# An encoder layer with a mixture of experts: one weight load and three row loads are issued at other places of the DMA queue

## The chip, the cores and the metric

One Trainium2 chip; the kernel runs on one of its cores. The time is what the device takes for one execution, in microseconds (us); of several runs the median is given. The core has a tensor engine (PE in the rows, PEld for its weight loads), a vector engine (DVE), a scalar engine (ACT), GpSimd (POOL) and SyncE (SP). In this kernel SP does no arithmetic: it issues DMAs, in the order of its own program, each after the waits that stand ahead of it. POOL issues the DMAs that gather and scatter rows by an index. "Slot" below is one of three places in the on-chip memory that hold the weights of one expert.

## The reference

One layer over two groups of tokens, 512 and 256, each token 1024 wide, float32. What matters here is its last part: a second RMS norm, a router that picks one of 4 groups and two of the 8 experts in it, the 32 SwiGLU experts, a gated residual, and the last RMS norm.

```
h = rms_norm(x, norm2_g) * (1 + sc2) + sh2
gsel = argmax(softmax(h @ rg_w + rg_b))            # one group of 4
top_p, top_i = top_k(softmax(le of that group), 2)  # two experts of its 8
eid = gsel * 8 + top_i                              # 768 tokens, 2 picks each
for each expert e:
    xb = h[tokens of e]
    y = (silu(xb @ w1[e]) * (xb @ w3[e])) @ w2[e]   # w1, w3: 1024x512, w2: 512x1024
    out[token] += weight * y
x = x + g2 * out
return rms_norm(x, final_g)
```

Ahead of it stand the first norm, the input projection, neighbourhood attention on one half of the width, a bidirectional RWKV-7 recurrence on the other, and the output projection.

## The kernel before, in words

The program is written by hand, engine by engine: each engine has one list of instructions per phase, and semaphores alone set the order between engines. Phases 4 to 7 follow each other in one block without a barrier, so an engine walks from one to the next as soon as its own list lets it.

Phase 5 (`sp_phase5`, `dve_phase5`, `pe_phase5`) ends the output projection, makes the second norm, writes the normed rows to the DRAM scratch `h2_dram`, and turns the router's scores into index lists by a long chain of small DVE operations (L2103 to L2182). When `idx_ready` comes (L2159), POOL may gather; when the last weight of a pick is made (L2182), `list_ready` comes, and SP writes the overflow lists to DRAM (L2000 to L2002).

Phase 6 goes over the 32 experts. Each has room for 64 rows. For expert e POOL gathers its 64 rows from `h2_dram` (L2363); PE transposes them (L2459), ACT copies them out of PSUM (L2403); PE multiplies with w1 and then w3 (both L2472), ACT and DVE make the gated product, PE transposes it (L2481) and multiplies with w2 (L2490); DVE copies the result (L2442), and POOL scatters it to DRAM (L2352). The first two gathers wait for nothing but the index; gather e waits until the rows of expert e-2 are transposed.

Each expert has three weights of 2 MB. There are three slots (`NSLOT = 3`), so nine weights can be loaded before any of them is used. Phase 5 issues these nine on SP between its other transfers: `weights(n, slot)` at L1965, n being 0 for w1, 1 for w3, 2 for w2. Of slot 2 the weights 0 and 1 are issued before SP waits for `list_ready`, and weight 2 behind the lists (L2003 in the code, shown at L1965). From then on (`ahead`, L2326) SP loads a weight of expert e+3 as soon as PE has used the same weight of expert e: `sp.wait_ge(sem(name), CREDIT + c.n + 1)`. All these transfers stand in SP's one queue.

Three rows of the last stage, each spread over all 128 partitions (512 KB of writes), are issued at L2342 (`g2_row`, two of them) and L2343 (`f_row`, the final norm's gain), after the loop, once w2 of expert 29 has been used.

Phase 7 reads the scattered results back (L2525, six loads of 1 MB), joins them on PE and DVE, norms, and writes the output (L2528).

Memory is one `arena`, cut by a counter `top[0]`. Slot 2 lies from `ARENA - 2 * WEXP` on. The routing temporaries (`both_e`, `rank16`, `level` and others) are taken one after another from `at_gate` on, and before the change some of them lie in slot 2's region of w2; hence its load stands behind `list_ready`, the end of their use.

Of the kernel before, what the change touches and what calls it, by code (L numbers as in the profile page):

```python
# [21 lines left out]
f16 = mybir.dt.float16  # L22
# [6 lines left out]
P = 128  # L29
D = 1024  # L30
# [3 lines left out]
NT = NT_S + NT_P  # L34
TOK = NT * P
# [9 lines left out]
NE, EPG, NG = 32, 8, 4  # L45
HID = 512
KH = HID // P
BLK = 64
MAX_OVER = 2 * TOK // BLK
NBLK = NE + MAX_OVER  # L50
# [102 lines left out]
def build(nc, A, O, upto=4):  # L153
    ctx = ExitStack()
    with ctx:
# [4 lines left out]
        def sem(name):  # L160
            if name not in sems:
                sems[name] = nc.alloc_semaphore(name=name)
            return sems[name]
# [5 lines left out]
        ARENA = 53200  # L169
        arena = ctx.enter_context(nc.sbuf_tensor("arena", [P, ARENA], f32))  # L170
        top = [0]

        def take(n):
            at = top[0]
            top[0] += n
            assert top[0] <= ARENA, top[0]
            return arena[:, at:at + n]
# [11 lines left out]
        mod_dram = dram("mod_scratch", [2, 6 * D])  # L189
# [13 lines left out]
        at_gate = top[0]  # L203
# [879 lines left out]
        at_prep = top[0]  # L1083
# [785 lines left out]
        g2_row = take(2 * D).rearrange("p (g d) -> p g d", g=2)  # L1869
# [6 lines left out]
        WEXP = 2 * KD * HID + KH * D  # L1876
# [33 lines left out]
        top6 = top[0]  # L1910
# [19 lines left out]
        rank_row, block_row, token_row = part(BLK), part(NBLK), part(2 * NT)  # L1930
        thresholds = part(NE)[0:NE, 0:TOK // BLK - 1]
        half_place = part(1)
        counting = take(P + 1).bitcast(f16)
        before16, ones16 = counting[:, 0:P], counting[:, P:2 * P]
        tri16 = take(NE).bitcast(f16)[0:NE]
        at_both = top[0]
        shifted = arena[:, at_both:at_both + 2 * KD * 36].rearrange("p (g k e) -> p g k e", g=2, k=KD)
        ones32 = hT[:, 4, W:W + P]
        assert at_both + 2 * KD * 36 <= at_gate + NT_S * W, (at_both - at_gate)
        gm, gsum, m1, m2, pk = (take(NT) for _ in range(5))  # L1940
        og, tg = (take(NT * NG).rearrange("p (t g) -> p t g", g=NG) for _ in range(2))
        s8, t8, o1, o2 = (take(NT * 8).rearrange("p (t e) -> p t e", e=8) for _ in range(4))
        N2 = 2 * NT
        both_e = take(N2 * NE).rearrange("p (k t e) -> p k t e", k=2, t=NT)
        tmp_e = arena[:, top6:top6 + N2 * NE].rearrange("p (n e) -> p n e", e=NE)
        wrap = take(NBLK)
        lsel = take(NT * NE).rearrange("p (t e) -> p t e", e=NE)
        hits16 = take(NT * NE // 2).bitcast(f16).rearrange("p (t e) -> p t e", e=NE)
        rank12, first12, excl12, pos12, low12, base12 = (take(N2) for _ in range(6))
        level = take(N2 * (TOK // BLK - 1)).rearrange("p (n m) -> p n m", n=N2)  # L1950
        rank16 = take(N2 * BLK // 2).bitcast(f16).rearrange("p (n s) -> p n s", n=N2)
        block16 = take(N2 * NBLK // 2).bitcast(f16).rearrange("p (n b) -> p n b", n=N2)
        cnt_col, over_col = take(1), take(1)
        over_lvl = take(TOK // BLK)[0:NE, 0:TOK // BLK - 1]
        over16 = take(P // 2).bitcast(f16)[0:NE]
        sums = take(2 * NE)
        o32 = take(NE)
        assert top[0] <= at_prep, top[0]

        WEIGHTS = (("h1_mm", w1_f, w1_v), ("h3_mm", w3_f, w3_v), ("y_mm6", w2_f, w2_v))  # L1960

        def sp_phase5(sp):
            def weights(n, slot_no):
                name, slot, view = WEIGHTS[n]
                sp.dma_start(slot[slot_no], view[slot_no]).then_inc(sem(f"{name}_w{slot_no}"), 16)  # L1965

            def h2_rows(t):
                sp.wait_ge(sem("h2_ready"), t + 1)
                sp.dma_start(h2_dram[t * P:(t + 1) * P, :], h2[t % 2]).then_inc(sem(f"h2_out{t % 2}"), 16)

            sp.wait_ge(sem("rec_tr"), NT_S)
            for dst, src in ((route, A["c_route"]), (counting[:, 0:2 * P], A["c_counting"]), (tri16, A["c_tri16"])):
                sp.dma_start(dst, src).then_inc(sem("consts5_in"), 16)
            sp.wait_ge(sem("y_mm"), STEPS)
            x_rows(sp, 2)
            sp.wait_ge(sem("ss_ready"), 2)
            x_rows(sp, 3)
            h2_rows(0)
            for n in range(3):
                weights(n, 0)  # L1980
            for t in range(NT_S, NT):
                sp.wait_ge(sem(f"rec_tok{t}"), 1)
            for t in range(NT_S, NT):
                x_rows(sp, t)
            sp.wait_ge(sem("router_mm"), 1)
            weights(2, 1)
            for t in range(1, NT - 1):
                h2_rows(t)

            sp.wait_ge(sem("o5_mm"), 2 * NT)  # L1990
            weights(0, 1)
            h2_rows(NT - 1)
            weights(1, 1)
            weights(0, 2)
            sp.wait_ge(sem("router_mm"), NT)
            for q in range(2):
                sp.wait_ge(sem(f"h2_out{q}"), 48)
            weights(1, 2)
            sp.wait_ge(sem("list_ready"), 1)
            sp.dma_start(over_dram, lst_i[0:MAX_OVER, :]).then_inc(sem("list_out"), 16)  # L2000
            sp.dma_start(slot_dram.rearrange("(b s) o -> b (s o)", s=BLK), over_idx[NE:NBLK]).then_inc(sem("list_out"), 16)
            sp.dma_start(put_dram.rearrange("(b s) o -> b (s o)", s=2 * BLK), over_put[NE:NBLK]).then_inc(sem("list_out"), 16)  # L2002
            weights(2, 2)  # L2003

        def pool_phase5(pool):
            pool.wait_ge(sem("h2_out0"), 48)
# [257 lines left out]
        CREDIT = 3  # L2264
# [54 lines left out]
        def sp_phase6(sp):  # L2319
            def ahead(c):  # L2320

                static = isinstance(c.n, int)
                if not static or c.n + NSLOT < NE:
                    for name, slot, view in WEIGHTS:
                        sp.wait_ge(sem(name), CREDIT + c.n + 1)
                        sp.dma_start(slot[c.w], one(view, c.e + NSLOT)).then_inc(sem(f"{name}_w{c.w}"), 16)  # L2326

            turns(sp, ahead, ahead=NSLOT)

            def over(c):  # L2330
                sp.wait_ge(sem("over_done"), c.n + 1)
                sp.dma_start(idx_o[0:BLK, :], slot_dram[bass.ds(c.first_slot, BLK), :]).then_inc(c.sem("idx_in0"), 16)
                sp.dma_start(put_o, put_dram[bass.ds(c.first_slot * 2, 2 * BLK), :]).then_inc(c.sem("idx_in0"), 16)
                for name, slot, view in WEIGHTS:
                    sp.dma_start(slot[0], one(view, c.e)).then_inc(c.sem(f"{name}_w0"), 16)


            sp.wait_ge(sem("list_out"), 48)
            count = overflow_count(sp)
            sp.wait_ge(sem("y_mm6"), CREDIT + NE - 2)  # L2340
            for g in range(2):
                sp.dma_start(g2_row[:, g, :], mod_dram[g, 5 * D:6 * D].partition_broadcast(P)).then_inc(sem("g2_in"), 16)  # L2342
            sp.dma_start(f_row, A["final_row"].partition_broadcast(P)).then_inc(sem("final_in"), 16)  # L2343
            sp.wait_ge(sem("y_mm6"), CREDIT + NE)
            overflow(sp, over, count, with_expert=True)

# [159 lines left out]
        top[0] = ARENA - WEXP  # L2506
        yo = [take(D) for _ in range(NT)]
        top[0] = ARENA - 2 * WEXP
        f_row = take(D)
        sq7 = take(D)  # L2510
        stat7 = take(NT * 4).rearrange("p (t m) -> p t m", t=NT)

# [171 lines left out]
```

## Time and profile before

| what | us |
|---|---|
| median of 3 runs | 1383.43 |
| lowest, highest | 1381.2, 1383.94 |
| span of the profiled execution, first to last instruction | 1375.9 |
| around the span, to the median | 7.5 |
| phase 5's end: last gather before the experts issued at | 825.70 |
| experts: first matmul with w1, last matmul group with w2 | 830.59, 1329.71 |
| mean granted clock of the tensor engine | 0.948 |

The profiled execution's own device time is not among the recorded ones; 7.5 us is the median of the runs less the span. Times in the rows count from the span's start. From 840 to 1320 us, a third of the whole, the DMA engines are busy all the time at some 400 GB/s. Before that there are a few microseconds in which they carry next to nothing.

### The profile page before, as it was taken

Reading aid. Unit: us, or ns where it says so; the run is one execution under the profiler, and the core shown is the slowest. Engines: PE = TensorE matmul, PEld = TensorE weight load, DVE = VectorE, ACT = ScalarE, POOL = GpSimd, SP = SyncE. Lnnn points to the kernel's source line nnn. Section 1 sums busy time; section 2 is a strip of 40 time slices with the busy share of each in tenths; the row PEclk is TensorE's granted clock in tenths of the full one; section 3 lists DMA queues with packets and bytes.
Section 4 is the critical chain, followed back from the end, with each engine's and each line's share of the span. In section 5 each row is a group of like instructions: output and inputs, shape, how many; then the busy total and the mean of one; then the engine's idle time right before and its main releaser. Section 6 shows DMA issues by size and latency. Waiting matters only on the chain.

```text
span 1375.9 us, 29721 instructions
## 1 busy us (share of the span) xinstructions
PE 1178.5 (86%) x13063; PEld 727.2 (53%) x13063; DVE 421.8 (31%) x742; ACT 348.6 (25%) x749; POOL 280.7 (20%) x254
## 2 busy tenths in 40 slices
PE   5899999999997898988899958997788878888765
PEld 3555555555454787877755535554444444444432
DVE  2100043434565555666437361000000000000017
ACT  3200024353323554565532111110010010010003
POOL 0100012221326343367412001111111111111000
PEclk9999999999997899999999978999999999999987
DMA  9894231122435211221407169999999999999966
GB/s 319 325 337 164 69 94 62 54 82 72 153 123 141 68 39 38 50 57 27 172 7 310 70 262 327 398 390 397 401 404 405 408 404 404 398 395 396 411 270 249
DMA packets 82025, 314.74 MB, mean 229 GB/s; under 512 B 13808, under 2 KB 28488, under 8 KB 65150
## 3 DMA queue, kind: packets, MB, share of 16 engines
q1 hardware_dynamic: 75862, 298.96, 58.5%
q0 software_dynamic: 5120, 12.59, 2.6%
q8 instruction: 87, 1.43, 0.4%
q10 hardware_dynamic: 936, 1.61, 0.3%
q14 instruction: 20, 0.16, 0.0%
HBM read 291.58 MB, written 25.74 MB: 231 GB/s over the span
## 4 chain that ended last, share of the span: by engine, by line
PE 28%; DMA 27%; DVE 5%; ACT 4%; issue 3%; SPq 1%; POOL 0%; DVEq 0%; POOLq 0%; ACTq 0%
DMA arena<-in_exp_w 26%; PE bank L1585 10%; PE bank L2472 6%; PE bank L1855 6%; PE bank L2490 2%; PE bank L1609 2%; SPq L2326 1%; DVE arena L1466 1%; PE bank L2211 1%; PE bank L2459 1%; DMA arena<-pick_out 1%; DVE arena L1453 1%; DVE arena L2577 0%; ACT arena L1295 0%; DVE arena L1483 0%
## 5 line engine op out<-in xcount | busy, mean ns | idle before, releaser
L2472 PE MATMUL bank<-arena 128*64 128x256 f32 x2048 | 256.8, 409 | 67.9 <-DMA arena<-in_exp_w 58.1
L907 PE MATMUL bank<-arena 128*128 128x512 f32 (+1 forms) x736 | 256.3, 497 | 4.4 <-POOL arena L493 1.6
L2472 PEld LDWEIGHTS bank<-arena 128*64 128x64 f32 x2048 | 158.7, 147 | 175.4 <-DMA arena<-in_exp_w 70.0
L1585 PE MATMUL bank<-arena 64*64 64x64 f16 (+3 forms) x7184 | 204.7, 221 | 36.4 <-issue 12.6
L1585 PEld LDWEIGHTS bank<-arena 64*64 64x64 f32 (+2 forms) x7184 | 183.2, 127 | 63.6 <-issue 35.9
L907 PEld LDWEIGHTS bank<-arena 128*128 128x128 f32 x736 | 133.9, 189 | 99.4 <-issue 85.0
L2490 PE MATMUL bank<-arena 128*64 128x512 f32 x512 | 118.6, 605 | 17.5 <-ACT arena L2416 17.5
L2438 DVE TENSOR_TENSOR arena<-bank,arena 128x256 f32<-128x256 f32 x32 | 13.6, 424 | 303.5 <-PE bank L2472 303.5
L2363 POOL DMA_INDIRECT arena<-h_scratch,arena x32 | 30.8, 962 | 362.5 <-PE bank L2459 260.7
L1855 PE MATMUL bank<-arena 128*128 128x512 f32 x192 | 86.4, 597 | 0.0
L2490 PEld LDWEIGHTS bank<-arena 128*64 128x64 f32 x512 | 34.8, 137 | 79.3 <-issue 55.7
L2442 DVE COPY arena<-bank 128x512 f32<-128x512 f32 x32 | 22.1, 692 | 167.0 <-PE bank L2490 167.0
L2403 ACT COPY arena<-bank 128x512 f32<-128x512 f32 x32 | 18.8, 586 | 205.8 <-PE bank L2459 205.8
L2352 POOL DMA_INDIRECT pick_out<-arena x32 | 32.4, 1014 | 173.9 <-DVE arena L2442 173.9
L2410 ACT ACTIVATE arena<-bank 128x256 f32<-128x256 f32 x32 | 12.3, 384 | 208.7 <-PE bank L2472 208.7
L1855 PEld LDWEIGHTS bank<-arena 128*128 128x128 f32 x192 | 34.9, 189 | 37.9 <-issue 37.3
L450 POOL TENSOR_TENSOR arena<-arena 128x512 f32<-128x512 f32 x16 | 16.7, 1042 | 161.5 <-DVE arena L778 161.5
L1479 DVE CAST arena<-bank 128x512 f16<-128x512 f32 x48 | 32.9, 686 | 39.4 <-PE bank L1585 39.4
L942 PE MATMUL bank<-arena 128*128 128x512 f32 x96 | 42.9, 598 | 0.0
L735 DVE COPY arena<-bank 128x512 f32<-128x512 f32 (+1 forms) x8 | 4.5, 559 | 113.8 <-PE bank L907 113.8
L2459 PEld LDWEIGHTS bank<-arena 64*128 64x128 f32 x256 | 30.7, 199 | 16.4 <-issue 16.4
L2459 PE MATMUL bank<-arena 64*128 64x64 f32 x256 | 35.0, 278 | 4.4 <-DMA arena<-h_scratch,arena 4.4
(262 smaller groups left out, 1285.9 us busy)
## 6 DMA issues: line engine op xcount, KB each, us to landing
arena<-in_exp_w SPq DMA_DIRECT2D x96, 2048.0 KB, 44.7
arena<-in_ada_w SPq DMA_DIRECT2D x12, 2048.0 KB
arena<-in_w_in SPq DMA_DIRECT2D x11, 1024.0 KB, 6.6
direction_scratch<-arena SPq DMA_DIRECT2D x6, 1536.0 KB, 5.9
arena<-direction_scratch SPq DMA_DIRECT2D x24, 384.0 KB, 5.4
arena<-pick_out SPq DMA_DIRECT2D x6, 1024.0 KB, 10.1
arena<-in_x_sample SPq DMA_DIRECT2D x8, 512.0 KB, 5.0
arena<-in_w_out SPq DMA_DIRECT2D x8, 512.0 KB, 6.4
```

Source lines behind the costliest of these rows:

```text
L907: return nc.tensor.matmul(bank[i % 3][:, 0:GR[p] * GW], w[:, k, :], hT[:, k, PART[p]], start=(k == 0), stop=(k == KD - 1))
L942: ins = nc.tensor.matmul(bank[i % 3], hT[:, k, c * P:(c + 1) * P], wv[:, k, :], start=(k == 0), stop=(k == KD - 1))
L1479: nc.vector.tensor_copy(nm[1 + l % 2][:, 1], bank[6].rearrange("p (j r c) -> p j r c", j=NPAIR, r=2)).then_inc(sem("nm_dve"), 1)
L1585: return nc.tensor.matmul(out, lhsT, r, start=start, stop=True, skip_group_check=True)
L1609: ins = nc.tensor.transpose(bank[q % 2][:, j * P:(j + 1) * P], src[:, j * P:(j + 1) * P], ident)
L1855: ins = nc.tensor.matmul(out_bank(t, hf), catT[:, k, t * P:(t + 1) * P], wout[k][:, hf * 512:hf * 512 + 512], start=(k == 0), stop=(k == K ...
L2352: nc.gpsimd.indirect_dma_start(y_dram, bass.IndirectOffsetOnAxis(ap=put_all.bitcast(u32)[:, e:e + 1], axis=0), yb[e % 2], None, bounds_che ...
L2363: nc.gpsimd.indirect_dma_start(xg[e % 2][0:BLK, :], None, h2_dram, bass.IndirectOffsetOnAxis(ap=idx_all.bitcast(u32)[0:BLK, e:e + 1], axis=0),
L2442: nc.vector.tensor_copy(yb[c.s], bank[6 + c.s]).then_inc(c.sem("y_ready6"), 1)
L2459: ins = nc.tensor.transpose(bank[0][:, j * BLK:(j + 1) * BLK], xg[c.s][0:BLK, j::KD], ident[0:BLK, 0:BLK])
L2472: ins = nc.tensor.matmul(bank[b + 2 * c.s][BLK * n:BLK * n + BLK, 0:HALF], xT[c.s][:, j, :], slot[c.w][:, j, n * HALF:(n + 1) * HALF], sta ...
L2490: ins = nc.tensor.matmul(bank[6 + c.s][BLK * n:BLK * n + BLK, :], hidT[:, j % 2, j // 2, :], w2_s[c.w][:, j, n * 512:(n + 1) * 512], start ...
```

## The change

The routing temporaries are laid out anew: some go into the room of the scatter buffers in front of `top6`, the others behind `tmp_e`, and none of them reaches slot 2 any more (two asserts say so). No DVE, ACT, PE or POOL instruction is added, removed or put elsewhere in its engine's order. On SP, weight 2 of slot 2 is issued before the wait for `list_ready`, and the three rows of the last stage right behind the lists; at their old place, and with them the wait for expert 29, they are gone. `f_row` gets a place of its own in front of slot 2, free from then on.

```diff
--- before.py
+++ after.py
@@ -1930,32 +1930,38 @@
         rank_row, block_row, token_row = part(BLK), part(NBLK), part(2 * NT)
         thresholds = part(NE)[0:NE, 0:TOK // BLK - 1]
         half_place = part(1)
-        counting = take(P + 1).bitcast(f16)
+        counting = take(P).bitcast(f16)
         before16, ones16 = counting[:, 0:P], counting[:, P:2 * P]
         tri16 = take(NE).bitcast(f16)[0:NE]
         at_both = top[0]
         shifted = arena[:, at_both:at_both + 2 * KD * 36].rearrange("p (g k e) -> p g k e", g=2, k=KD)
         ones32 = hT[:, 4, W:W + P]
         assert at_both + 2 * KD * 36 <= at_gate + NT_S * W, (at_both - at_gate)
-        gm, gsum, m1, m2, pk = (take(NT) for _ in range(5))
-        og, tg = (take(NT * NG).rearrange("p (t g) -> p t g", g=NG) for _ in range(2))
-        s8, t8, o1, o2 = (take(NT * 8).rearrange("p (t e) -> p t e", e=8) for _ in range(4))
+        assert at_both <= ARENA - 2 * WEXP
         N2 = 2 * NT
-        both_e = take(N2 * NE).rearrange("p (k t e) -> p k t e", k=2, t=NT)
         tmp_e = arena[:, top6:top6 + N2 * NE].rearrange("p (n e) -> p n e", e=NE)
-        wrap = take(NBLK)
+
+        top[0] = top6 - 2 * HID
         lsel = take(NT * NE).rearrange("p (t e) -> p t e", e=NE)
         hits16 = take(NT * NE // 2).bitcast(f16).rearrange("p (t e) -> p t e", e=NE)
-        rank12, first12, excl12, pos12, low12, base12 = (take(N2) for _ in range(6))
-        level = take(N2 * (TOK // BLK - 1)).rearrange("p (n m) -> p n m", n=N2)
         rank16 = take(N2 * BLK // 2).bitcast(f16).rearrange("p (n s) -> p n s", n=N2)
         block16 = take(N2 * NBLK // 2).bitcast(f16).rearrange("p (n b) -> p n b", n=N2)
         cnt_col, over_col = take(1), take(1)
         over_lvl = take(TOK // BLK)[0:NE, 0:TOK // BLK - 1]
+        assert top[0] <= top6
+        top[0] = top6 + N2 * NE
+        gm, gsum, m1, m2, pk = (take(NT) for _ in range(5))
+        og, tg = (take(NT * NG).rearrange("p (t g) -> p t g", g=NG) for _ in range(2))
+        s8, t8, o1, o2 = (take(NT * 8).rearrange("p (t e) -> p t e", e=8) for _ in range(4))
+        both_e = take(N2 * NE).rearrange("p (k t e) -> p k t e", k=2, t=NT)
+        wrap = take(NBLK)
+        rank12, first12, excl12, pos12, low12, base12 = (take(N2) for _ in range(6))
+        level = take(N2 * (TOK // BLK - 1)).rearrange("p (n m) -> p n m", n=N2)
         over16 = take(P // 2).bitcast(f16)[0:NE]
         sums = take(2 * NE)
         o32 = take(NE)
-        assert top[0] <= at_prep, top[0]
+        assert top[0] <= at_gate, top[0]
+        f_row = arena[:, ARENA - 2 * WEXP - D:ARENA - 2 * WEXP]
 
         WEIGHTS = (("h1_mm", w1_f, w1_v), ("h3_mm", w3_f, w3_v), ("y_mm6", w2_f, w2_v))
 
@@ -1996,11 +2002,14 @@
             for q in range(2):
                 sp.wait_ge(sem(f"h2_out{q}"), 48)
             weights(1, 2)
+            weights(2, 2)
             sp.wait_ge(sem("list_ready"), 1)
             sp.dma_start(over_dram, lst_i[0:MAX_OVER, :]).then_inc(sem("list_out"), 16)
             sp.dma_start(slot_dram.rearrange("(b s) o -> b (s o)", s=BLK), over_idx[NE:NBLK]).then_inc(sem("list_out"), 16)
             sp.dma_start(put_dram.rearrange("(b s) o -> b (s o)", s=2 * BLK), over_put[NE:NBLK]).then_inc(sem("list_out"), 16)
-            weights(2, 2)
+            for g in range(2):
+                sp.dma_start(g2_row[:, g, :], mod_dram[g, 5 * D:6 * D].partition_broadcast(P)).then_inc(sem("g2_in"), 16)
+            sp.dma_start(f_row, A["final_row"].partition_broadcast(P)).then_inc(sem("final_in"), 16)
 
         def pool_phase5(pool):
             pool.wait_ge(sem("h2_out0"), 48)
@@ -2337,10 +2346,6 @@
 
             sp.wait_ge(sem("list_out"), 48)
             count = overflow_count(sp)
-            sp.wait_ge(sem("y_mm6"), CREDIT + NE - 2)
-            for g in range(2):
-                sp.dma_start(g2_row[:, g, :], mod_dram[g, 5 * D:6 * D].partition_broadcast(P)).then_inc(sem("g2_in"), 16)
-            sp.dma_start(f_row, A["final_row"].partition_broadcast(P)).then_inc(sem("final_in"), 16)
             sp.wait_ge(sem("y_mm6"), CREDIT + NE)
             overflow(sp, over, count, with_expert=True)
 
@@ -2506,7 +2511,6 @@
         top[0] = ARENA - WEXP
         yo = [take(D) for _ in range(NT)]
         top[0] = ARENA - 2 * WEXP
-        f_row = take(D)
         sq7 = take(D)
         stat7 = take(NT * 4).rearrange("p (t m) -> p t m", t=NT)
 
```

SP's list at the end of phase 5, before. `in_exp_w` is the experts' weights, a row with `128x4096` is a w1 or w3, one with `128x2x2048` a w2; `overflow_list`, `slot_token` and `slot_place` are the lists in DRAM; the wait for `list_ready` stands ahead of the first of them.

```order
L1969 DMA h_scratch<-arena 128x1024
L1965 DMA arena<-in_exp_w 128x4096 x3
L2000 DMA overflow_list<-arena 24x2
L2001 DMA slot_token<-arena 24x64
L2002 DMA slot_place<-arena 24x128
L1965 DMA arena<-in_exp_w 128x2x2048
L2299 UNCONDITIONAL_BRANCH
```

The same place now. `mod_scratch` holds the two `g2` rows, `in_final_row` the final gain.

```order
L1975 DMA h_scratch<-arena 128x1024
L1971 DMA arena<-in_exp_w 128x4096 x3
L1971 DMA arena<-in_exp_w 128x2x2048
L2007 DMA overflow_list<-arena 24x2
L2008 DMA slot_token<-arena 24x64
L2009 DMA slot_place<-arena 24x128
L2011 DMA arena<-mod_scratch 128x1024 x2
L2012 DMA arena<-in_final_row 128x1024
L2308 UNCONDITIONAL_BRANCH
```

The w2 of slot 2 moved from behind the lists to ahead of them, and three row loads stand where it stood.

SP's list behind the loop over the experts, before:

```order
L2326 DMA arena<-in_exp_w 128x2x2048
L2308 TENSOR_LOAD overflow_list
L2308 ISA x2
L2342 DMA arena<-mod_scratch 128x1024 x2
L2343 DMA arena<-in_final_row 128x1024
L2312 COMPARE_AND_BRANCH
```

and now:

```order
L2335 DMA arena<-in_exp_w 128x2x2048
L2317 TENSOR_LOAD overflow_list
L2317 ISA x2
L2321 COMPARE_AND_BRANCH
L2322 UNCONDITIONAL_BRANCH
```

The three row loads left this place; nothing took it.

## Rows read from the trace of the kernel before

**Rows 1.** The page: the span, and GB/s moved in its 40 slices.
```profile
span 1375.9 us, 29721 instructions
...
GB/s 319 325 337 164 69 94 62 54 82 72 153 123 141 68 39 38 50 57 27 172 7 310 70 262 327 398 390 397 401 404 405 408 404 404 398 395 396 411 270 249
```

**Rows 2.** The chain that ended last: start us, us, what.
```profile
824.25 4.23 DMA arena<-h_scratch,arena
828.61 1.12 PE bank L2459 x8
...
830.59 8.61 PE bank L2472 x64
...
1279.48 44.74 DMA arena<-in_exp_w
1324.27 3.70 PE bank L2472 x32
...
1329.71 3.67 PE bank L2490 x16
...
1338.23 7.18 DMA arena<-pick_out
```

**Rows 3.** Stretches: length, five engines' busy time, PE clock, DMA share, GB/s.
```profile
820.00:824.00 4.00, 2.12 (x47) 2.15 (x48) 2.15 (x9) 0.00 (x0) 0.00 (x0) 0.50 0.96 410
826.00:830.00 4.00, 1.11 (x8) 0.95 (x8) 1.19 (x9) 0.68 (x3) 0.66 (x1) 0.50 0.38 108
836.00:838.00 2.00, 2.00 (x22) 1.33 (x20) 0.00 (x0) 1.54 (x2) 0.00 (x0) 1.00 1.02 295
840.00:1320.00 480.00, 397.01 (x2724) 221.16 (x2725) 33.57 (x61) 43.33 (x96) 58.19 (x59) 0.95 1.01 401
1325.00:1330.00 5.00, 3.74 (x32) 2.22 (x30) 0.42 (x1) 0.37 (x1) 0.00 (x0) 1.00 0.50 205
```

**Rows 4.** SP's transfers in order of time: start us, us, line.
```profile
811.59 0.33 SPq L1965 DMA_DIRECT2D arena<-in_exp_w  x1
...
827.88 0.32 SPq L2000 DMA_DIRECT2D overflow_list<-arena  x1
...
829.22 0.41 SPq L1965 DMA_DIRECT2D arena<-in_exp_w  x1
835.94 125.92 SPq L2326 DMA_DIRECT2D arena<-in_exp_w  x28
...
1302.31 0.81 SPq L2342 DMA_DIRECT2D arena<-mod_scratch  x2
```

**Rows 5.** Weight loads issued at 811.59, 829.22, 835.94, 1285.1 us: time to landing.
```profile
DMA to landing us min/median/max: 14.5/14.5/14.5
DMA to landing us min/median/max: 10.1/10.1/10.1
DMA to landing us min/median/max: 8.2/8.2/8.2
DMA to landing us min/median/max: 44.5/44.5/44.5
```

**Rows 6.** Weight load issued at 802.05 us, and the row loads: KB, us to landing.
```profile
arena<-in_exp_w SPq DMA_DIRECT2D x1, 2048.0 KB, 8.2
arena<-mod_scratch SPq DMA_DIRECT2D x2, 512.0 KB, 25.3
arena<-in_final_row SPq DMA_DIRECT2D x1, 512.0 KB, 30.2
```

**Rows 7.** Gathers issued at 824.25 and 830.49 us, then the 29 later ones.
```profile
arena<-h_scratch,arena POOLq DMA_INDIRECT x1, 4.2
arena<-h_scratch,arena POOLq DMA_INDIRECT x1, 8.2
DMA to landing us min/median/max: 7.5/9.1/10.3
```

## The prediction

> **What bounds the kernel now.** I read the page first. The slices of 34 us show a last third in which about 400 GB/s are moved, with two slices at the end below that, and ahead of it slices with far less [rows 1]. The chain of waits says what this stretch is: from the middle of it on, PE takes a weight, SP issues the next load into the freed slot, and the data is there 45 us later [rows 2]. The stretch table confirms that throughput sets this: from 840 to 1320 us the DMA share is 1.01 at 401 GB/s, while PE is busy for 397 of 480 us [rows 3]. A load of 2048 KB (2.097 MB) costs 2.097 MB / 401 GB/s = 5.2 us of all DMA engines, and no hole in it waits for another engine once the stream has begun. Its end therefore moves with its beginning, and with its bytes.
>
> So I read the beginning step by step in the same chain. DVE's routing chain ends in the index; POOL issues gather 0 at 824.25, its 64 rows are there 4.23 us later, PE transposes them at 828.61, ACT copies, and the matmuls of w1 and w3 of expert 0 start at 830.59 [rows 2]. After the w1 half SP issues the first load of the stream, w1 of expert 3, at 835.94 [rows 4]; it lands after 8.2 us [rows 5], at 844.1. That one load is bound by expert 0's w1 matmuls, and through them by the landing of gather 0. Everything behind it queues.
>
> The end: the last w3 lands at 1324.2, PE uses it, and w2 follows at 1329.71; then come the last scatter and the read-back, whose first tile is there 7.18 us after 1338.23 [rows 2].
>
> **Part 1: the w2 of slot 2 ahead of the list.** Before, it is issued at 829.22 and lands at 839.3 [rows 4, 5]. Now it is issued right behind the w3 of slot 2, which goes out at 811.59 and lands at 826.1 [rows 4, 5]. The engines are full until about then (share 0.96 at 820 to 824) and nearly idle in 826 to 830 (0.38, 108 GB/s) [rows 3]. The load fills that hole: it starts at about 826 and ends at 826.1 + 5.2 = 831.3, or with gathers 0 and 1 in its way (64 rows of 4 KB each, 0.26 MB, 0.65 us each) at 832.6. Its issue, 0.4 us, falls into SP's wait for the list, from 811.9 to 827.88. Nobody needs this weight before expert 2, so its earlier landing is worth nothing in itself.
>
> What it costs is in that same hole. Gather 0 found the DMA engines all but empty: 4.2 us to landing. Gather 2, issued 1.3 us behind the very load that is moved, took 8.2, and the 29 others, all inside the stream, 7.5 to 10.3 with a median of 9.1 [rows 7]. Now gather 0 meets the load too. Bounds for its delay: 0 from below, if the load is no obstacle; from above it can't be later than the end of the load with the two gathers, 832.6, since behind that the engines are free, so 832.6 - 828.5 = 4.1 us. Durations from the rows give 7.5 - 4.2 = 3.3 (shortest of the loaded gathers), 8.2 - 4.2 = 4.0 (gather 2), 9.1 - 4.2 = 4.9 (median, beyond the cap). I take 3.3, because a part of the load is through when the gather's data is due, while the gathers of 9 us met loads queued one behind the other. PE has nothing else to do then (1.11 us busy of 826 to 830 [rows 3], all of it expert 0's transposes), so its start slips by all of it, and with it ACT's copy, both matmul halves of expert 0, and SP's wait at 835.94, behind which every further weight load stands. The Trainium skill says the same of the sharing, "Trainium Kernel Development and Optimization", Key Constraints: DMAs of SP, ACT and POOL run on the same 16 engines and interleave, so the gather's own queue does not shield it. By that rule the load is not free in the hole; the trace agrees, with 4.2 against 7.5 to 10.3 us.
>
> What could be given back: with the queue empty, w1 of expert 3 might land faster. Before, it was issued with 3.3 us of the moved load still to land (839.3 - 835.94), and took 8.2 us [rows 4, 5]. The first load of phase 5 at 802.05, which found the engines empty, also took 8.2 [rows 6]. So the gain is 0 by these two rows; at most it is the 0.65 us of gather 2, which stood in the way too (the share was 1.02 at 836 to 838, without a hole [rows 3]). I take 0.3.
>
> **Part 2: three rows behind the lists.** 3 x 512 KB = 1.57 MB, 3.9 us of the DMA engines. They are issued at about 829.3 to 830.5 and run behind the moved load: 832.6 + 3.9, and gather 2 with 0.65, ends at 837.2. In the likeliest case the first load of the stream is issued at 835.94 + 3.3 = 839.2, behind them: cost 0. If gather 0 is not delayed, that load is issued at 835.94 and its data could flow from about 837 on: cost 0 to 1 us. SP's time for the three issues lies in its wait for PE.
>
> **Part 3: the rows gone from the tail.** They were issued at 1302.31 and landed after 25.3 (median of two) and 30.2 us, the last at about 1333.4 [rows 4, 6], before the read-back with whose data DVE needs them is on its way (1338.23 [rows 2]). SP issues nothing between them and that read-back. Had they held up the last weights, their going would give up to 3.9 us. But at 1325 to 1330 the DMA share was 0.50 [rows 3]: engines stood idle while the last weight was still landing, and in one queue the rows stood behind it. I take 0, with the 3.9 as a bound.
>
> **Part 4: the temporaries.** The same DVE instructions with the same shapes at other addresses; DVE's chain from 802 to 828 has no row that depends on the address. 0.
>
> **Sum.** +3.3 (gather 0) - 0.3 (first load) + 0 + 0 + 0 = +3.0 us. The profiled span of 1375.9 would be 1378.9; the median of the runs lies 7.5 above the span of before, so 1383.4 + 3.0 = 1386.4.
>
> **The rivals.**
> A, the gather is hardly delayed: the load gets between its packets, but the wait is 0 to 1.5 us. For it: the hole is short and half of the load is through. Against: none of the 30 gathers that met a load took under 7.5 us [rows 7]. The change would then be 0 to +1.5, less 0.3: about 1384.0.
> B, the gather waits for the whole load. For it: gather 2 landed at 838.7 and the load, issued ahead of it, at 839.3, nearly together [rows 5, 7]. The delay is then the cap, 4.1 us, less 0.3: 1387.2. The Trainium skill, "DMA: Bandwidth & Descriptors", Queues, rings and completion order, has a rule that comes to this: a DMA engine changes between queues only after a whole packet, typically 9 to 17 descriptors of one ring. It would make the gather wait for most of the load; the trace leaves it open, because gather 2 met the load only from its start on.
> C, the other side: the tail is freed. The rows' packets share single DMA engines with the last weights of expert 31, and the tail ends earlier when they are gone. Price up to 3.9 us; with the delayed gather 1386.4 - 3.9 = 1382.5, without it 1383.4 - 3.9 = 1379.5. It decides once the last w2 lands less than 40.6 us instead of 44.5 us behind its issue [rows 5]. For it: the rows' landings (the two of 25.3 us in median) fall into the time of the last two weights. Against: the half-idle engines.
> D, nothing that can be measured happens: the w1 load of expert 3 had been bound by the moved load and not by PE, so that an empty queue gives 2 to 3 us back and cancels the gather's delay. For it: the share of 1.02 at 836 to 838. Against: 8.2 us with and without a queue ahead. About 1384.
>
> **How the numbers follow.** Forecast and B together are one mechanism: 0.40 and 0.17. A 0.20, D 0.13, C 0.10. A measurement of this kernel can tell about 0.2%, 2.8 us, from no change. The forecast's +3.0 lies just beyond that, so two thirds of its chance count as slower (0.27), one third as same (0.13). B is slower by 0.15 and same by 0.02. A and D are same but for 0.01 each of faster. C gives 0.06 faster, 0.04 same. Sum: faster 0.08, same 0.50, slower 0.42. The range takes in B with a microsecond of spread above it, and A, D and C's nearer end below: 1382.3 to 1388.3; the forecast's own is 1385 to 1387.5.
>
> **What would show it.** The hole at 826 to 830 us should be filled to over 300 GB/s. Gather 0's transfer should take 7 to 8 us instead of 4.2, PE's first transposes start at 831 to 833 instead of 828.61, and w1 of expert 3 be issued at about 839 instead of 835.94. The stream from there on should be as long as before: from that issue to the last w2 matmuls 1329.7 - 835.9 = 493.8 us, within a microsecond. In the tail there should be no row loads, and the same 7 us to the first tile. The prediction is wrong if gather 0 still lands within 5.5 us (A), or if those 493.8 us shrink by over 2 us (C or D), or if the stream starts later and the last weights don't come later.

## The result and the profile after

The changed kernel takes 1390.32 us in the median of 22 runs (1386.57 to 1394.33); the kernel before, in 22 runs on the same chips, 1384.7 (1380.69 to 1392.5). The ratio is 1.003, with a 95% interval of 1.0019 to 1.0041: slower by 4.2 us (2.6 to 5.7). The direction and the place were as predicted. The forecast of +3.0 lies in that interval, but the measured median lies outside the range given for it: 2.0 us above its upper end of 1388.3. Of the 6.9 us between the 1383.43 that the prediction started from and 1390.32, 1.3 are the median of before itself, which rose to 1384.7 with more runs. The rest, 5.6 us between the medians and 4.2 by the ratio, is the change, and a part of it was sized too small.

The profiled execution spans 1384.8 us, 8.9 more than before, which is more than the ratio says. The chain of waits of the changed kernel (start us, us, what) tells where it comes from:

```profile
824.79 0.87 DVE arena L2164
825.79 0.83 PE bank L2259 x12
827.33 0.58 issue
828.15 9.58 DMA arena<-h_scratch,arena
837.87 1.12 PE bank L2464 x8
839.01 0.59 ACT arena L2408
839.85 8.71 PE bank L2477 x64
...
1332.41 3.70 PE bank L2477 x32
...
1337.85 3.67 PE bank L2495 x16
...
1346.38 7.46 DMA arena<-pick_out
```

Against [rows 2], gather 0 is issued 3.90 us later (828.15 for 824.25). Of the change, only the new addresses of the temporaries and the issue of the w2 load (815.94) lie ahead of that. Already the w3 load of slot 2, ahead of that issue in SP's order, goes out 3.97 us later (815.56 for 811.59), and in three later kernels without an early load gather 0 is issued at 828.5, 828.9 and 830.4. So the 3.90 us are taken as a difference between single executions and set aside here. The profiled execution of before was a short one. Around the changed kernel's span lie 2.0 us (1386.79 less 1384.8), and not 7.5; with 2.0 the execution of before would have taken 1377.9, an estimate, and none of its 22 runs was below 1380.69. Then gather 0 takes 9.58 us instead of 4.23: 5.35 us, and expert 0 starts by as much later. The further stretches in the table below are the first stream load to the last scatter, and from there to the end of the span. In the list of SP's transfers (start us, us) the first stream load stands at 845.30, in [rows 4] at 835.94:

```profile
810.15 6.22 SPq L1971 DMA_DIRECT2D arena<-in_exp_w  x4
831.78 0.32 SPq L2007 DMA_DIRECT2D overflow_list<-arena  x1
832.15 0.37 SPq L2008 DMA_DIRECT2D slot_token<-arena  x1
832.56 0.36 SPq L2009 DMA_DIRECT2D slot_place<-arena  x1
832.96 0.83 SPq L2011 DMA_DIRECT2D arena<-mod_scratch  x2
833.83 0.43 SPq L2012 DMA_DIRECT2D arena<-in_final_row  x1
845.30 9.31 SPq L2335 DMA_DIRECT2D arena<-in_exp_w  x3
```

| stretch, us | before | after | difference |
|---|---|---|---|
| start to the issue of gather 0 | 824.25 | 828.15 | +3.90, not the change's |
| gather 0 to the first stream load | 11.69 | 17.15 | +5.46 |
| first stream load to the last scatter | 498.93 | 497.71 | -1.22 |
| last scatter to the end | 41.03 | 41.79 | +0.76 |

The last three sum to +5.0, inside the interval of the ratio. The last two are no larger than the differences, in the same stretches, between the profiles of the variants below whose loads there are the same. The hole is filled. Stretches of the changed kernel (length, five engines' busy time, PE clock, DMA share, GB/s), the first to be held against the 108 GB/s of [rows 3]:

```profile
826.00:830.00 4.00, 2.15 (x48) 2.01 (x45) 2.44 (x14) 0.00 (x0) 1.54 (x2) 0.50 0.97 414
834.00:836.00 2.00, 0.00 (x0) 0.00 (x0) 0.00 (x0) 0.00 (x0) 0.00 (x0) 0.50 1.05 211
842.00:1320.00 478.00, 398.25 (x2750) 223.10 (x2748) 33.50 (x60) 44.12 (x96) 58.20 (x59) 0.95 1.00 396
```

The second line is one that the prediction didn't foresee: while the two gathers, the w2 load, the lists and the rows are under way together, the engines are busy all the time (1.05) and move half of what they can (211 GB/s). PE does nothing at all there. When the gathers get going is told by the DMA queues: q0 is the gathers' queue, q1 SP's (packets, MB, share of the engines; no line for q0 where none of its packets ran). Before, in 824.30 to 826.05 and in 826.05 to 828.60:

```profile
q1 hardware_dynamic: 21, 0.08, 11.4%
```
```profile
q0 software_dynamic: 156, 0.41, 54.2%
```

In the changed kernel, in 828.20 to 832.40 and in 832.40 to 833.00:

```profile
q1 hardware_dynamic: 213, 1.71, 97.1%
```
```profile
q1 hardware_dynamic: 21, 0.17, 81.3%
q0 software_dynamic: 14, 0.05, 22.8%
```

The first packet of a gather runs 1.8 us behind gather 0's issue before, and only some 4.3 us behind it now, after SP's queue has moved 1.71 MB. So about 2.5 of the 5.35 us pass before any row of a gather moves, and the rest while rows and load share the engines. From issue to landing (us), of the w3 and the moved w2 load of slot 2, and of gather 0:

```profile
DMA to landing us min/median/max: 14.6/14.6/14.6
DMA to landing us min/median/max: 22.6/22.6/22.6
```
```profile
arena<-h_scratch,arena POOLq DMA_INDIRECT x1, 9.6
```

The w3 load took 14.5 before [rows 5], and lands at 830.2 here; the w2 load, issued 0.4 us behind it (815.94), lands at 838.5, and gather 0 at 837.7, 0.8 us ahead of it.

### The profile page after: what moved, and what is told of

It is laid out like the page before. It is cut to its first block, busy times and chain, and to the rows that moved or that the text cites. A ratio compares the mean times of both kernels' runs of the same rounds, so it can differ in the third digit from the quotient of the medians.

```text
span 1384.8 us, 29721 instructions
## 1 busy us (share of the span) xinstructions
PE 1176.7 (85%) x13063; PEld 724.3 (52%) x13063; DVE 421.5 (30%) x742; ACT 348.6 (25%) x749; POOL 280.7 (20%) x254
## 4 chain that ended last, share of the span: by engine, by line
PE 28%; DMA 28%; ACT 5%; DVE 5%; issue 3%; POOL 0%; DVEq 0%; SPq 0%; POOLq 0%; ACTq 0%
DMA arena<-in_exp_w 26%; PE bank L1585 10%; PE bank L2477 7%; PE bank L1855 6%; PE bank L2495 2%; PE bank L1609 2%; PE bank L2220 1%; DMA arena<-h_scratch,arena 1%; DVE arena L1466 1%; PE bank L2464 1%; DVE arena L1453 1%; DMA arena<-pick_out 1%; ACT arena L1295 1%; DVE arena L2581 0%; ACT arena L1285 0%
## 5 line engine op out<-in xcount | busy, mean ns | idle before, releaser
L1585 PE MATMUL bank<-arena 64*64 64x64 f16 (+3 forms) x7184 | 199.4, 218 | 41.5 <-issue 15.9
L1585 PEld LDWEIGHTS bank<-arena 64*64 64x64 f32 (+2 forms) x7184 | 178.3, 125 | 68.2 <-issue 39.9
L2464 PEld LDWEIGHTS bank<-arena 64*128 64x128 f32 x256 | 30.6, 199 | 21.8 <-issue 21.8
```

Source lines behind the costliest of these rows:

```text
L1585: return nc.tensor.matmul(out, lhsT, r, start=start, stop=True, skip_group_check=True)
L2464: ins = nc.tensor.transpose(bank[0][:, j * BLK:(j + 1) * BLK], xg[c.s][0:BLK, j::KD], ident[0:BLK, 0:BLK])
```

## The experiments

Each was timed in five rounds beside the kernel before on the same chip (6 runs of the kernel with only the rows moved, 8 to 12 of the others, 24 to 31 of before); a ratio is to the kernel before in the same rounds. Every cut of code is against the changed kernel, with `...` for what is left out. "Stream" is the series of weight loads from w1 of expert 3 on. Three numbers are read from each profile, since they are free of what happens ahead of gather 0: how long gather 0 takes, the time from its issue to that of the first stream load (A), and from there to the last scatter (B).

| kernel | ratio (95%) | gather 0 | A | B |
|---|---|---|---|---|
| before | 1 | 4.2 | 11.69 | 498.93 |
| changed | 1.0030 (1.0019 to 1.0041) | 9.6 | 17.15 | 497.71 |
| w2 early, rows in the tail | 1.0043 (1.0026 to 1.0061) | 9.3 | 17.81 | 498.60 |
| w2 early, lists and rows behind the gathers | 1.0037 (1.0021 to 1.0053) | 8.9 | 16.63 | 500.58 |
| half of w2 early, rows in the tail | 1.0032 (1.0018 to 1.0045) | 6.3 | 15.27 | 497.98 |
| rows only | 1.0054 (1.0035 to 1.0073) | 4.2 | 11.69 | 503.03 |
| layout only | 0.9999 (0.9985 to 1.0013) | 4.1 | 12.98 | 497.91 |
| w2 in the earlier hole | 1.0008 (0.9994 to 1.0021) | 4.3 | 12.49 | 497.42 |
| same, w1 loads in halves | 0.9996 (0.9979 to 1.0013) | 4.2 | 10.17 | 501.53 |
| order of before, w1 loads in halves | 1.0001 (0.9985 to 1.0018) | 4.0 | 9.96 | 503.07 |
| earlier hole, every sixth w1 in halves | 1.0007 (0.9991 to 1.0024) | 4.1 | 9.72 | 501.68 |
| earlier hole, PE kept at work | 0.9991 (0.9971 to 1.0012) | 4.1 | 10.06 | 499.61 |
| the last two together | 0.9997 (0.9976 to 1.0018) | 4.2 | 8.43 | 501.69 |

**Only the w2 load early.** The rows go back to the tail.

```diff
             sp.dma_start(put_dram..., over_put[NE:NBLK]).then_inc(sem("list_out"), 16)
-            for g in range(2):
-                sp.dma_start(g2_row[:, g, :], ...)
-            sp.dma_start(f_row, ...)
...
+            sp.wait_ge(sem("y_mm6"), CREDIT + NE - 2)
+            for g in range(2): ...
```

> The w2 load of slot 2 ahead of the list as in the changed kernel, the three row loads back at the tail. Theory T1 (the moved load alone delays gather 0, and with it the whole weight stream): gather 0 takes 9 us or more as in the changed kernel (9.6), the first stream load is issued some 17 us behind gather 0 instead of 11.7, and the time is 4 to 5 us above the kernel before, as the changed kernel is. Theory T2 (the load alone costs only about 3 us, the lists and the rows queued behind it stretch the gather beyond it): gather 0 takes 7 to 8 us, the time is 2 to 3 us above before, and the moved load lands about 17 us after its issue instead of 22.6. Rival T3 (the gather is no matter, the row loads cost their bytes in the stream): the time is that of before.

Gather 0 takes 9.3 us, A is 17.8 us, and the moved load lands after 21.8: T1, and not T2. The ratio of 1.0043 is +6.0 us (3.6 to 8.4), with T1's 4 to 5 inside, and T3 falls. The cost is there without the rows behind the lists.

**Only the rows behind the lists.** The w2 load stands between the lists and the rows.

```diff
             weights(1, 2)
-            weights(2, 2)
             sp.wait_ge(sem("list_ready"), 1)
             ...
+            weights(2, 2)
             for g in range(2):
```

> The w2 load of slot 2 back behind the lists, the three row loads right behind it and no longer in the tail. T1 and T2 agree: gather 0 takes 4.2 us as before, PE starts expert 0 as before, but the rows (1.57 MB, 3.9 us) now lie between the w2 load and the first load of the stream, which lands 12 us behind its issue instead of 8.2: 3 to 4 us above the kernel before. If the tail gained from the missing rows (up to 3.9 us, rival C of the prediction), the time is that of before, and the last w2 lands less than 41 us behind its issue instead of 44.5.

Gather 0 takes 4.2 us, and A is the 11.69 us of before to the hundredth. The first stream load waits behind the rows:

```profile
arena<-in_exp_w SPq DMA_DIRECT2D x1, 2048.0 KB, 14.9
```

14.9 us for 8.2 [rows 5], somewhat more than the 12 expected, and B grows by 4.1 us. The ratio says +7.5 us (4.8 to 10), the medians +4.4; the 3.9 us of bytes lie just below the interval. So the rows cost about their bytes where they stand in the stream's way. In the changed kernel they don't: the last of them, issued at 833.83, lands after 9.2 us, at 843.0, and the first stream load is issued at 845.30. A part of this room is the gather's delay. Without it, 11.69 us behind gather 0, that issue would stand at 839.8, an estimate, with rows still under way. The tail gives nothing back: the last w2 lands 41.9 us behind its issue, 43.3 in the changed kernel and 44.5 before [rows 5], none below the 40.6 that the prediction's rival C needed.

**Lists and rows behind the gathers.** SP waits for the landing of gathers 0 and 1 before it issues lists and rows, so gather 0 meets the w2 load and nothing else.

```diff
             sp.wait_ge(sem("list_ready"), 1)
+            sp.wait_ge(sem("xg_in0"), 16)
+            sp.wait_ge(sem("xg_in1"), 16)
```

> The changed kernel, but SP waits for the landing of gathers 0 and 1 before it issues the lists and the rows, so that gather 0 meets the w2 load and nothing else. T1: gather 0 takes 9 to 10 us as in the changed kernel, time as that of the changed kernel (4 to 5 us above before). T2: gather 0 takes 7 to 8 us, the w2 load lands about 17 us after its issue, and the time is 2.5 to 3.5 us above before.

Gather 0 takes 8.9 us and the load lands after 22.8, as late as in the changed kernel. T2 falls: with lists and rows held back only 0.7 us of the gather's time are gone, of the 1.6 to 2.6 that T2 wanted. Three rows of this kernel's stretches show the cause at work alone:

```profile
832.00:834.00 2.00, 0.00 (x0) 0.00 (x0) 0.00 (x0) 0.00 (x0) 0.00 (x0) 0.50 1.00 307
834.00:836.00 2.00, 0.00 (x0) 0.00 (x0) 0.00 (x0) 0.00 (x0) 0.00 (x0) 0.50 0.60 143
836.00:838.00 2.00, 1.11 (x8) 0.95 (x8) 0.00 (x0) 0.04 (x1) 0.00 (x0) 0.50 0.04 14
```

When gathers and load mix, the rate falls with full engines (1.00, 307 GB/s); then the share falls too (0.60, and 0.04), while gather 0 lands only at 836.6 and the load at 837.8. The reading that fits is that some engines are through early and the gather waits for the last one's part; no row here tells the engines apart. B is 1.7 us longer, since the rows, issued late, again stand ahead of the first stream load (11.1 us to landing).

**Half the obstacle.** Only the first half of the w2 load stands ahead of the list.

```diff
-            weights(2, 2)
+            sp.dma_start(w2_f[2][:, 0:1], w2_v[2][:, 0:1]).then_inc(sem("half_in"), 16)
             sp.wait_ge(sem("list_ready"), 1)
             ...
+            sp.wait_ge(sem("half_in"), 16)
+            sp.dma_start(w2_f[2][:, 1:2], w2_v[2][:, 1:2]).then_inc(sem("y_mm6_w2"), 16)
```

> Half of the obstacle: of the w2 load of slot 2 only the first half (1 MB) is issued ahead of the list, the second behind it; rows in the tail. T1 (gather 0 waits for what of the load stands ahead of it): the half load ends 2.6 us behind the w3 before it, so gather 0 takes 5.5 to 7 us, between 4.2 and the 9.3 to 9.6 with the whole load, and the time is 1 to 2.5 us above before. Rival P (a gather that meets any queued load pays the same 4 to 5 us, as all 30 loaded gathers took 7.5 us and more): gather 0 takes 8 us or more, 4 us above before.

The gather follows the dose: 6.3 us, between 4.2 and 9.3, so P falls. The half load (issued at 821.86, 17.6 us to landing) is there at 839.5, and gather 0 at 840.4, 0.9 us behind it. The time doesn't follow as neatly: 4.4 us above before (2.5 to 6.2), where 1 to 2.5 were expected; A and B of the one profile together say +2.6. A grew by 3.6 us, 2.1 by the gather and 1.5 by PE, whose first 64 matmuls took longer here than before. Profile before, then this kernel, start us and us:

```profile
830.59 8.61 PE L2472 MATMUL bank<-arena 128*64 128x256 f32 x64 [0.87 <-ACT arena L2403]
```
```profile
842.56 10.07 PE L2480 MATMUL bank<-arena 128*64 128x256 f32 x64 [0.87 <-ACT arena L2411]
```

The granted clock goes from 0.50 to 1.00 at 833.6 in the first, 3 us into these matmuls, and at 848.5 in the second, 6 us into them. They took 8.5 to 10.1 us over the kernels in which PE stands idle before them. The new layout alone has 10.02 there (A 12.98) and is as fast as before, so this is no cost of an edit; it is a reason not to read A to better than 1.5 us from one profile.

**Only the layout.** The order of before, with the new places.

```diff
             weights(1, 2)
-            weights(2, 2)
             sp.wait_ge(sem("list_ready"), 1)
             ...
+            weights(2, 2)
-            for g in range(2): ...
-            sp.dma_start(f_row, ...)
```

> The new places of the routing temporaries and of the gain row, with SP's order as in the kernel before (w2 of slot 2 behind the lists, the rows in the tail). T1: nothing is left of the cost, ratio to before 1.000 within its interval, gather 0 in 4.2 us, 11.7 us from gather 0 to the first stream load. Rival L (the layout costs by itself, in DVE's chain or in the tail): 1.002 or more.

0.9999 (0.9985 to 1.0013), gather 0 in 4.1 us: the places of the temporaries cost nothing that could be measured, and rival L falls. A is 12.98 and not the 11.7 expected, by the slower matmuls just shown.

**The w2 load in the earlier hole.** It goes out right behind the fourth tile's normed rows. The rows of the last stage stay behind the lists.

```diff
-            weights(2, 2)
...
-            for t in range(1, NT - 1):
-                h2_rows(t)
+            for t in range(1, NT_S):
+                h2_rows(t)
+            weights(2, 2)
+            for t in range(NT_S, NT - 1):
+                h2_rows(t)
```

> The w2 load of slot 2 is issued right behind the fourth tile's normed rows, some 40 us ahead of the gathers, where the DMA engines are nearly idle; the row loads stand behind the lists as in the changed kernel. T1 and T2: gather 0 lands in 4.2 us again, the rows run in the hole behind it (issued at about 829, done by 834) and the first stream load finds an empty queue: time within 1 us of before, rather 0.3 to 0.7 us below it. T3 or any cost of the rows by themselves: 3 to 4 us above before.

In this kernel SP issues (start us, us):

```profile
780.46 0.32 SPq L1975 DMA_DIRECT2D h_scratch<-arena  x1
780.82 0.44 SPq L1971 DMA_DIRECT2D arena<-in_exp_w  x1
796.85 0.32 SPq L1975 DMA_DIRECT2D h_scratch<-arena  x1
```

Gather 0 is back at 4.3 us, the rows run behind it, and the ratio is 1.0008 (0.9994 to 1.0021), against the changed kernel's 1.0030 (1.0019 to 1.0041). With an early load and the same early rows, the cost is gone, within 2.9 us, once the load is through before the gather. It also shows that the hoped-for gain of 0.3 to 0.7 us isn't to be seen: the first stream load lands in 7.8 us instead of 8.2, but with only the layout changed, and the order of before, it took 7.5.

**Making the stream begin earlier.** If its end follows its beginning, a version faster than both should be within reach. Five kernels were tried, the second of them as a control that keeps the order of before. First, each w1 load is issued as two halves, the first when PE has used half of the old weight:

```diff
-                    for name, slot, view in WEIGHTS:
+                    for cols, name in zip(W1_HALVES, ("h1_half", "h1_mm")):
+                        sp.wait_ge(sem(name), CREDIT + c.n + 1)
+                        sp.dma_start(w1_f[c.w][:, cols], one(w1_v, c.e + NSLOT)[:, cols])...
+                    for name, slot, view in WEIGHTS[1:]:
```

> As the kernel with the w2 load in the earlier hole and the rows behind the lists, and every w1 load issued as two halves of 1 MB, the first as soon as PE has used the first four of the eight parts of the same weight three experts earlier. If the stream's end follows its beginning (T1's footing), the first half goes out some 2.5 us earlier into an empty queue and the time is 2 to 3 us below before (ratio 0.998 to 0.9985), gather 0 staying at 4.2 us. If the beginning is not what sets the end, or the further DMAs cost issue time, it is the time of before or above.

> The order of the kernel before, with only the w1 loads split in halves as in the other kernel of this job. The w2 load of slot 2 still stands in the queue until some 10 us behind its issue, so the half that is released 2.5 us earlier finds it ahead: less than 1 us below before, ratio 0.9995 to 1.000. If it gains as much as the kernel with the emptied queue (2 to 3 us), the emptied queue is worth nothing.

The first missed its gain: 0.9996 (0.9979 to 1.0013) where 0.998 to 0.9985 was expected. The control, for which 0.9995 to 1.000 was expected, has 1.0001 (0.9985 to 1.0018). The first half load goes out 10.2 and 10.0 us behind gather 0, but B is 501.5 and 503.1 us. That w1 now moves in smaller pieces was one explanation; the stream from 900 to 1300 us runs at 398 GB/s in the first of them:

```profile
900.00:1300.00 400.00, 322.46 (x2213) 179.13 (x2212) 27.49 (x49) 35.90 (x79) 49.19 (x50) 0.94 1.01 398
```

Halves only for every sixth expert keep the pieces of the others:

```diff
+                        if name == "h1_mm" and c.q == 0:
+                            for cols, used in zip(W1_HALVES, ("h1_half", "h1_mm")):
+                                ...
```

> As the kernel with the w2 load in the earlier hole, with w1 loads in two halves for every sixth expert only, the first of the stream among them, so that 24 of the 29 w1 loads keep their 16 KB pieces. If the smaller pieces ate the gain when all w1 loads were split (398 GB/s in the stream instead of 400 to 401), the time is now 1.5 to 2.5 us below before. If an earlier first load doesn't move the end, it is that of before.

1.0007, B 501.7, and 398 GB/s over the same stretch (400 in the earlier hole with whole loads): no gain, so the pieces of the later loads are not the explanation. SP's list (start us, us) shows how little came earlier. It is that of this kernel, with gather 0 issued at 828.60:

```profile
838.32 2.05 SPq L2341 DMA_DIRECT2D arena<-in_exp_w  x2
843.35 0.33 SPq L2344 DMA_DIRECT2D arena<-in_exp_w  x1
```

The second half goes out 1.7 us behind the first, and the load of w3, which waits for expert 0's w3 matmuls, 14.8 us behind gather 0; before, with a whole w1 load, it was 15.0 (839.24). In the other two with halves it is 16.4 and 15.6. So the halves bring 1 MB forward and nothing behind it. Next, nine matmuls keep PE at work while gather 0 is under way:

```diff
+            for j in range(WARM):          # 9
+                nc.tensor.matmul(bank[6][:, 0:P], ident, ident, start=True, stop=True)
             rows(Main(0, 0, 0, 0, 0, 0))
```

> As the kernel with the w2 load in the earlier hole, and nine 128x128 matmuls of the identity matrix put in front of expert 0's transposes, into a bank that nobody reads then; they run in the 4 us in which PE waits for gather 0. PE stands at 0.50 granted there and gets its full clock only 3 to 5 us into expert 0's matmuls. If the stream's end follows its beginning (T1's footing), the full clock comes earlier, the first stream load goes out 10 to 11 us behind gather 0 instead of 11.7 to 13, and the time is 1 to 2.5 us below before. If that footing is wrong, nothing changes: ratio 1.000.

The stretches show what it does to the granted clock (the number ahead of the DMA share), and the last row expert 0's 64 matmuls:

```profile
830.00:834.00 4.00, 0.78 (x15) 0.81 (x16) 2.79 (x9) 0.00 (x0) 0.00 (x0) 0.50 1.02 438
834.00:838.00 4.00, 4.00 (x53) 3.93 (x52) 2.73 (x16) 0.22 (x1) 2.10 (x2) 0.64 0.61 229
838.00:842.00 4.00, 1.71 (x14) 1.41 (x15) 0.80 (x5) 0.79 (x2) 0.32 (x2) 1.00 0.39 128
```
```profile
841.79 7.13 PE L2480 MATMUL bank<-arena 128*64 128x256 f32 x64 [0.87 <-ACT arena L2411]
```

With the filler PE is at 1.00 (2.4 GHz) before expert 0's matmuls begin, and these take 7.13 us instead of 8.5 and more at a clock of 0.50 (1.2 GHz) in part. A falls to 10.06, and the load of w3 goes out 13.4 us behind gather 0. The ratio is 0.9991 (0.9971 to 1.0012), the lowest of all, 1.2 us below before in the middle, but its interval includes 1. Both together:

> Both of the two others of this job. If both act on the stream's beginning: the first half load goes out about 9 us behind gather 0, and the time is 3 to 4 us below before (ratio 0.997 to 0.998). If only one acts, 1 to 2.5 us.

A is 8.43 us, the shortest, B 501.69, and the ratio 0.9997 (0.9976 to 1.0018). No version beats the kernel before beyond its interval.

## Why the prediction was right in its direction and too small

**The bound and the path.** Right. The moved load delays gather 0, expert 0 starts later, and the first stream load with it. From that load's issue to the last w2 matmuls it is 492.6 us (1337.85 less 845.30) for 493.8. A gather that doesn't meet the load (earlier hole, layout only) takes the cost away; one that meets only the load (lists and rows behind) keeps it.

**The delay of gather 0: the step that was mis-sized.** The prediction took 3.3 us, with 4.1 as the cap ("it can't be later than the end of the load with the two gathers"). Measured are 5.35 us, and 4.7 with lists and rows held back. Rival A, with 0 to 1.5 us, falls. Two things in the sizing failed.

It took the shortest of the loaded gathers because part of the load would be through by then. Being part of the way through did not help: no packet of a gather ran until some 4.3 us behind the issue, and gather 0 landed 0.8 us ahead of the load in the changed kernel (837.7 and 838.5) and 1.2 us ahead of it with lists and rows held back (836.6 and 837.8). This was rival B. Its packet rule (the Trainium skill, "DMA: Bandwidth & Descriptors", Queues, rings and completion order) would have a gather wait for most of the load that is queued when it comes. These landings agree with it, and so does the half load, which gather 0 followed by 0.9 us and where 6.3 us are 2.1 above the free gather.

And the cap itself did not hold. In the times of this execution it is 830.2 + 5.2 + 1.3 = 836.7, 8.5 us behind the gather's issue; the gather came 1.0 us later still. With only the lists behind the load it came 0.9 us behind its cap too (839.4 for 832.1 + 6.5); with lists and rows held back it came 0.3 us ahead of it (836.6 for 830.4 + 6.5, the w3 load having taken 15.8 us instead of 14.6). So the lists may have a part in the last microsecond; no run here separates that. The cap added up bytes at the full rate of 401 GB/s, while load and gathers together ran at 307 with nothing else issued, and at 344, 211 and 300 from 832 to 838 with lists and rows among them. The profile of before had shown this beside a number that the prediction did quote: 836 to 838, where gather 2 met the load, has a share of 1.02 and only 295 GB/s [rows 3]. It was read as "no hole", not as a slower rate.

**The gain of 0.3 at the first stream load.** The landing went from 8.2 to 8.1 us. B fell by 1.2 us in the changed kernel and by 0.3 with the rows in the tail; the size is within the spread of B over kernels with whole loads and no rows in the stream's way (497.4 to 499.6), so the 0.3 is neither confirmed nor refuted. Rival D, which needed 2 to 3 us here, is out, for the same landing of 8.1.

**The rows.** Right in both places: nothing in the changed kernel, where SP issued them by 834.3 and the first stream load came at 845.30; nothing from the tail. Rival C falls with the last w2 landing 43.3 us behind its issue, where it needed less than 40.6. The bytes were sized about right as well: 3.9 expected, 4.1 in B where they are in the way, though the ratio there says 4.8 to 10.

**The temporaries.** 0 expected, 0.9999 measured.

**The total.** With 5.35 in place of 3.3 the prediction's own sum is +5.1; the ratio says +4.2 (2.6 to 5.7) and the three stretches +5.0. As a range it missed because its upper end was the cap less 0.3, with 1.1 us of spread, on a median of three runs that itself moved by 1.3. That +3.0 lies within the interval of the ratio is in part luck: the profile says that its largest term was 2 us short.

**What stays open.** A later beginning of the stream moved the end by about as much: A +5.46 with a ratio of +4.2 us, A +6.1 with +6.0, A +4.9 and B +1.7 with +5.1. An earlier one did not: A shorter by 1.5 to 3.3 us, and ratios of 0.9991 to 1.0007. In the kernels with halves B took back most of it or more than all (501.5 to 503.1, for 497.4 to 499.6 with whole loads), whether all w1 loads were split or one in six. A good part of that is how A is counted there: it ends with the first half load, while the load of w3 went out no earlier than before. From the w3 load to the last scatter it is 494.1 to 497.4 us with halves and without. With the filler the w3 load did go out 1.6 us earlier (13.4 for 15.0 behind gather 0); a gain of that size lies within the intervals of both ratios, so whether the end follows an earlier beginning isn't shown either way.

## What to carry to other kernels

A hole in the DMA engines is not free if something small and urgent uses it: here the 0.26 MB gather on which the next stage's start hangs. In this kernel the bulk load belonged into a hole that ends before such a transfer is issued (the same load 40 us earlier cost nothing that could be measured). A cap on a delay is to be worked out at the rate that mixed traffic shows in the profile, not at the rate of the stream.

## What was not expected of the hardware

A full DMA share is no sign of a full rate. With gathers of 4 KB rows and a load the engines were at 1.00 and 1.02 and moved 307 and 295 GB/s; with lists and rows among them they were at 1.05 and moved 211, half of the stream's 401. It doesn't even take a gather: in the kernel before, right behind the lists, the first 16 packets of the w2 load were all that ran for 2 us, with no packet of gather 2, issued at 830.49, among them (packets, MB and share of q1 in 830 to 832, then the stretch).

```profile
q1 hardware_dynamic: 16, 0.13, 102.7%
```
```profile
830.00:832.00 2.00, 1.41 (x8) 0.85 (x10) 0.00 (x0) 0.34 (x1) 0.93 (x1) 0.50 1.03 66
```

A share of 1.03 goes with 66 GB/s there. PE's first matmuls after an idle time differ by 1.6 us between kernels that are alike up to there (8.5 to 10.1 us for the same 64), with the granted clock rising from 0.50 to 1.00 at 3 or at 6 us into them. Nine small matmuls in the idle time bring them to 7.13, with the granted clock at 1.00 at their start.
